# Who writes the high parts of the attention outputs: ScalarE in the place of VectorE

## The chip, the cores and the metric

One program on one core of a Trainium2 chip. The metric is the device time of one execution in microseconds; the number given is the median of several runs. All arrays are float32. One core has the engines TensorE (PE in the rows; PEld is its weight load), VectorE (DVE), ScalarE (ACT), GpSimd (POOL) and SyncE (SP, which here only issues DMAs). Each runs its own list of instructions in the order in which the program gives them, and waits for another engine only at a semaphore.

## The reference, cut to what matters

Two transformer blocks over 256 tokens of width 1024. There are five attentions; in the kernel they are called diff (8 heads of the differential attention), cross (4 heads of width 256 over a memory), mema (4 heads of width 64 over a second memory), swa (12 heads of width 64, sliding window of 128 with sinks) and memb (4 heads of width 64). Between cross and mema lies a layer that gathers experts, some 650 us long. What is touched here is the last step of four of the attentions and the product behind it:

```python
def cross_attention(h, m, w_cq, w_ckv, w_co):
    ...
    logits = jnp.einsum('bshd,bmhd->bhsm', q, k).astype(jnp.float32) * (CROSS_HEAD_DIM ** -0.5)
    p = jax.nn.softmax(logits, axis=-1).astype(v.dtype)
    o = jnp.einsum('bhsm,bmhd->bshd', p, v).reshape(b, s, CROSS_HEADS * CROSS_HEAD_DIM)
    return o @ w_co
...
        h = h + jnp.concatenate([main_out, mem_out], axis=-1) @ w_out[l]
```

## The kernel before

The large products run in a split form: an operand a is kept as a high part (its rounding to the fast matmul type) and a low part (a less its high part), and three products, high by high, low by high and high by low, are summed. The weights come in 154 halves of 1 MB; for each half ScalarE makes w_hi (L534) and VectorE w_lo (L1331). The operands' parts lie in op_hi and op_lo.

An attention is written as one loop in each of three engines, over items i (heads), two items ahead with the scores (lag 2; diff has lag 1). The lists of one turn i are, in this order:

- TensorE: scores S(i+2) (L1043), product with the values O(i-1) (L1056), transposed probabilities T(i) (L1079). O(i-1) needs the copy of T(i-1) in SBUF.
- VectorE: normalise(i) (in swa L1483, then L1484 and twice L1487), maxima(i+2) (L1439, or in swa twice L1436 and then L1447), in some turns a filler (a w_lo in cross; take_queries, L1859 and L1863, in turns 0 and 2 of swa), then take(i-1): a copy of O(i-1) to op_hi (L1506), a wait for that copy on VectorE's own semaphore, and the difference into op_lo (L1507), which also frees the bank.
- ScalarE: the exponentials exps(i+2) (in swa L604 first, then L609, two), which need maxima(i+2), then turned(i) (L622), the copy of T(i) out of its bank.

Behind the loop comes the last take on VectorE. O, S and T share four banks of PSUM in a rotation (misc_bank). The output product that follows (L961: co, outa, outb) starts when every O of the attentions in front of it has been taken. Its first two halves of w_hi and w_lo are made ahead; ScalarE makes the third w_hi after its last turned.

In cross an item is 128 partitions by 512 numbers, in the other three 64 partitions by 256. In mema, swa and memb two heads share a tile of op_hi, one in the lower 64 partitions and one in the upper. The diff attention goes to o_diff and is not split here.

Of the kernel before, what the change touches and what calls it, by code (L numbers as in the profile page):

```python
# [13 lines left out]
ACT = mybir.ActivationFunctionType  # L14
AX = mybir.AxisListType

P = 128
D = 1024
S = 256
# [3 lines left out]
HEADS = 8  # L23
HD = 64
# [7 lines left out]
SWA_HEADS = 12  # L32
SWA_TILES = SWA_HEADS * HD // P
MEM_HEADS = 4
# [145 lines left out]
def build(nc, x_in, mem_in, mem2_in, wstream, experts, vecs_in, bc_in, final_g, rel_in, keys_in, pool_in,  # L180
# [3 lines left out]
    with ctx:  # L184
# [5 lines left out]
        def sem(name):  # L190
            sems[name] = ctx.enter_context(nc.semaphore(name))
            return sems[name]
# [7 lines left out]
        op_hi = sb("op_hi", [P, 2, KC, S], F32R)  # L200
# [38 lines left out]
        o_diff = part(0, KC, S)  # L239
# [92 lines left out]
        gfin_in = sem("gfin_in")  # L332
        pool_in_s = sem("pool_in_s")
        alibi_in = sem("alibi_in")
        out_s = sem("out_s")
        dve_chain = sem("dve_chain")
        act_chain = sem("act_chain")
# [48 lines left out]
        def misc_bank(key):  # L386
            return banks[4 + MISC[key] % 4]
# [7 lines left out]
        def wait_misc(eng, key):  # L395
            eng.wait_ge(misc_full, MISC_ORDER[key] + 1)
# [4 lines left out]
        def empty_misc(ins, key):  # L401
            ins.then_inc(misc_free[MISC[key] % 4], 1)
# [27 lines left out]


        IN_PSUM = ("cross", "mema", "swa", "memb")

        def seen_keys(kind, qb):

# [2 lines left out]
        UNIT0, ITEM0 = {}, {}  # L438
# [79 lines left out]
        def _(act):  # L518
# [8 lines left out]
            def high_parts(upto):  # L527

                for n in range(halves[0], min(upto, NHALF)):
                    act.wait_ge(raw_in[n % RAW], 16 * (n // RAW + 1))  # L530

                    if n >= HI:
                        act.wait_ge(half_done, n - HI + 1)
                    act.activation(w_hi[:, n % HI, :, :], raw[:, n % RAW, :, :], ACT.Copy).then_inc(hi_ready, 1)  # L534
                halves[0] = max(halves[0], upto)
# [80 lines left out]
            def turned(kind, i):  # L616
                wait_misc(act, ("T", kind, i))

                if i >= 2:
                    wait_misc(act, ("O", kind, i - 2))  # L620
                n = S + seen_keys(kind, 0)
                e = act.activation(prob_t[:, (ITEM0[kind] + i) % 2, 0:n], misc_bank(("T", kind, i))[:, 0:n], ACT.Copy)  # L622
                empty_misc(e, ("T", kind, i))

            def free_prob(kind, i, group):

                j = i - 4 // group
                if j >= 0:
                    wait_misc(act, ("T", kind, j))

            def attention(kind, items, group, lag, fill=()):
                start = halves[0]
                for i in range(min(lag, items)):
                    for g in range(group):
                        exps(kind, i * group + g)
                for i in range(items):
                    if i + lag < items:
                        for g in range(group):
                            free_prob(kind, i + lag, group)
                            exps(kind, (i + lag) * group + g)  # L640
                    if i < len(fill):

                        high_parts(start + 2 * (i + 1))
                        if fill[i]:
                            fill[i]()
                    turned(kind, i)

            def copy_lin(key, dst, scale=None):
                product(key)
# [14 lines left out]
            for j in range(4):  # L664
                product(("q", j))
                src = lin_bank(("q", j)).rearrange("p (a b) -> p a b", a=2)
# [84 lines left out]
            for l in range(2):  # L751
                key = ("mkr", "ab"[l])
# [115 lines left out]
            for j in range(4):  # L868
                d = raw2[:, 2 * j:2 * j + 2, :]
# [439 lines left out]
        def _(dve):  # L1309
            def do(ins):  # L1310

                chain(dve, ins, dve_chain)
# [174 lines left out]
                    dve.tensor_scalar(prob[:, r, qb, 0:n], prob[:, r, qb, 0:n], rsum[:, r, qb:qb + 1], None,  # L1487
                                      ALU.mult).then_inc(p_ready, 1)

            def attention(kind, items, group, lag, extra, dst, fill=(), lows=()):  # L1490
                for i in range(min(lag, items)):
                    for g in range(group):
                        maxima(kind, i * group + g, **extra(i * group + g))
                def take(i):

                    key = ("O", kind, i)
                    wait_misc(dve, key)
                    lo, hi, buf, d, w = dst(i)
                    src = misc_bank(key)[lo:hi, 0:w]
                    if w == 2 * S:  # L1500
                        src = rows2(src)
                    if buf is None:
                        empty_misc(dve.tensor_copy(o_diff[:, d, :], src), key)
                        return

                    do(dve.tensor_copy(op_hi[lo:hi, buf, d, :], src))  # L1506
                    empty_misc(dve.tensor_tensor(op_lo[lo:hi, buf, d, :], src,  # L1507
                                                 op_hi[lo:hi, buf, d, :].bitcast(F32), ALU.subtract), key)

                for i in range(items):  # L1510
                    normalise(kind, i)
                    if i + lag < items:
                        for g in range(group):
                            u = (i + lag) * group + g
                            j = i + lag - 4 // group
                            if j >= 0:
                                wait_misc(dve, ("T", kind, j))
                            maxima(kind, u, **extra(u))
                    if i < len(lows):
                        low_parts(lows[i])  # L1520
                    if i < len(fill) and fill[i]:
                        fill[i]()
                    if i < len(lows) and kind == "diff":
                        low_parts(lows[i] + 1)
                    if i:
                        take(i - 1)
                take(items - 1)


# [47 lines left out]
            def take_cb(i):  # L1577
                def f():
                    for j in (2 * i, 2 * i + 1):
# [5 lines left out]
                return f  # L1585

            attention("diff", HEADS, 2, 1, lambda u: dict(bias_ap=bias[:, u // 2]),
                      lambda h: (0, P, None, h, S),
                      [take_cc(0), take_cc(1), take_cb(0), take_cb(1)],
                      [LAST[("cx", 3)] + 2 * i + 2 for i in range(HEADS)])  # L1590
            for j in range(4):
# [37 lines left out]
            for j in range(4):  # L1629
# [8 lines left out]
            add_and_take("mixo", "cross", "cross", 1)  # L1638
            low_parts(LAST[("cq", 3)])
            attention("cross", CROSS_HEADS, 1, 2, lambda u: {},  # L1640
                      lambda h: (0, P, 0, slice(2 * h, 2 * h + 2), 2 * S),
                      lows=[LAST[("cq", 3)] + 1, LAST[("cq", 3)] + 2])
            add_and_take("co", "ffn", "ffn", 1)

# [161 lines left out]
                                                        op_hi[:, 1, t, :].bitcast(F32), ALU.mult, ALU.subtract),  # L1806
                               key)

            def half_tile(t0):

                def f(h):
                    lo = HD * (h % 2)
                    return lo, lo + HD, 1, t0 + h // 2, S
                return f

            attention("mema", MEM_HEADS, 1, 2, lambda u: {}, half_tile(SWA_TILES))

            def slope_diagonals():
                for u, h in enumerate(SWA_ORDER):
# [50 lines left out]
            def swa_extra(u):  # L1870
                h = SWA_ORDER[u]
                return dict(sink=bc[:, 4 * HD + h:4 * HD + h + 1])

            low_parts(LAST[("inb", 3)] + 2)
            attention("swa", SWA_HEADS, 1, 2, swa_extra, half_tile(0),
                      [lambda: take_queries(2), None, lambda: take_queries(3)])
            attention("memb", MEM_HEADS, 1, 2, lambda u: {}, half_tile(SWA_TILES))
            mlp("b")


# [96 lines left out]
```

## Time and profile before

| | us |
|---|---|
| median of 3 runs | 1784.98 (1779.49 to 1786.22) |
| the profiled execution: its own time | 1784.74 |
| the profiled execution: span | 1782.9 |
| the stretch of cross, first scores to first output product | 412.5 to 435.15 |
| the stretch of mema | 1230.7 to 1247.4 |
| the stretch of swa and memb | 1504.7 to 1569.7 |

The profile is of one execution. A row of its timeline gives the start, the length, engine, line, operation, tile out and in, the shapes and the count; in square brackets stands how long the engine had been idle and what ended that. A row that says x2 or x4 covers several instructions that followed one another. The granted clock of TensorE is given as a part of 2.4 GHz; it has two levels, 1.2 and 2.4 GHz, and a mean between 0.5 and 1 is a mix of the two. The time that lies around the span is 1.84 us.

### The profile page before, as it was taken

The page shows a single profiled execution, that of the slowest core. Times are in us where ns is not written, and L with a number is a line of the kernel's source. Part 1 is how long each engine was busy: PE and PEld are TensorE (multiplying, and loading weights), DVE is VectorE, ACT ScalarE, POOL GpSimd, SP SyncE. Part 2 cuts the span into 40 slices and gives each one's busy share as a digit, 9 for nine tenths or more (in the row PEclk, how much of TensorE's full clock was granted, in tenths as well). Part 3 has the DMA queues.
Part 4 walks back from the last instruction along what each step waited for, and adds up shares of the span by engine and source line. Part 5 has one row for each costly group of instructions (what it writes and reads, how often), then busy time and mean ns, then how long its engine had stood idle before and what let it go on. Part 6 is the DMA issues. An engine that isn't in the chain of part 4 may idle for free.

```text
span 1782.9 us, 20788 instructions
## 1 busy us (share of the span) xinstructions
PE 1533.8 (86%) x7994; PEld 1149.3 (64%) x7994; DVE 1090.5 (61%) x1953; ACT 741.1 (42%) x1372; POOL 250.0 (14%) x271
## 2 busy tenths in 40 slices
PE   7999999998997877777777777776999998789998
PEld 7998989987872322223232222264899887679987
DVE  5468645854576666676766665457544558744454
ACT  5534555443443334333333333233454355445532
POOL 0000000000033333333333333200000000000000
PEclk9999999999999999999999999988999999899999
DMA  7743444452489999999999999921355644024563
GB/s 249 248 164 142 159 140 171 154 179 74 168 334 422 421 421 421 421 421 421 421 417 421 421 409 421 385 73 61 142 177 181 196 161 142 1 82 180 188 192 116
DMA packets 70738, 442.10 MB, mean 248 GB/s; under 512 B 6983, under 2 KB 9295, under 8 KB 25200
## 3 DMA queue, kind: packets, MB, share of 16 engines
q0 software_dynamic: 36864, 268.45, 36.3%
q1 hardware_dynamic: 29904, 163.59, 26.5%
q10 hardware_dynamic: 3872, 8.75, 1.4%
q8 instruction: 63, 1.03, 0.2%
q14 instruction: 35, 0.29, 0.0%
HBM read 439.70 MB, written 2.63 MB: 248 GB/s over the span
## 4 chain that ended last, share of the span: by engine, by line
PE 56%; DMA 24%; DVE 11%; ACT 5%; issue 3%; POOL 0%; ACTq 0%; SPq 0%; DVEq 0%; PEldq 0%; POOLq 0%
PE banks L932 27%; DMA arena<-experts,xn 24%; PE banks L961 16%; PE banks L1204 7%; DVE w_lo L1331 3%; DVE arena L1716 2%; PE banks L1056 1%; PE banks L998 1%; PE banks L1043 1%; ACT xn L804 1%; DVE arena L1859 1%; ACT xn L808 1%; ACT op_hi L559 1%; ACT xn L797 1%; ACT w_hi L534 1%
## 5 line engine op out<-in xcount | busy, mean ns | idle before, releaser
L1204 PE MATMUL banks<-arena,xn 128*128 128x512 f32 x1024 | 478.0, 611 | 159.2 <-ACT xn L808 159.2
L1331 DVE TENSOR_TENSOR w_lo<-raw,w_hi 128x2048 fp32r<-128x2048 f32 x154 | 352.2, 2289 | 262.0 <-PE banks L932 128.7
L1204 PEld LDWEIGHTS banks<-arena,xn 128*128 128x128 f32 x1024 | 187.1, 192 | 449.3 <-ACT xn L808 258.6
L1716 DVE CUSTOM_DVE_ANT_0 arena<-arena,banks 128x1024 f32<-128x1024 f32 x256 | 312.2, 1220 | 214.9 <-DMA arena<-experts,xn 214.7
L534 ACT ACTIVATE w_hi<-raw 128x2048 fp32r<-128x2048 f32 x154 | 293.3, 1911 | 160.9 <-PE banks L961 133.1
L509 POOL DMA_INDIRECT arena<-experts,xn x256 | 242.8, 948 | 437.6 <-PE banks L1204 385.5
L932 PE MATMUL banks<-op_hi,w_hi 128*128 128x256 f32 x1520 | 220.5, 287 | 2.5 <-ACT op_hi L559 2.5
L932 PE MATMUL banks<-op_hi,w_lo 128*128 128x256 f32 x1520 | 214.4, 284 | 8.6 <-DVE w_lo L1331 8.6
L932 PE MATMUL banks<-op_lo,w_hi 128*128 128x256 f32 x1520 | 214.1, 284 | 0.0
L797 ACT ACTIVATE xn<-xn,stat 128x2 f32<-128x2 f32 x128 | 37.8, 295 | 403.5 <-DVE xn L1716 400.3
L932 PEld LDWEIGHTS banks<-op_hi,w_hi 128*128 128x128 f32 x1520 | 197.8, 192 | 8.3 <-ACT op_hi L559 4.8
L932 PEld LDWEIGHTS banks<-op_hi,w_lo 128*128 128x128 f32 x1520 | 196.0, 192 | 10.2 <-DVE w_lo L1331 10.2
L932 PEld LDWEIGHTS banks<-op_lo,w_hi 128*128 128x128 f32 x1520 | 196.9, 193 | 0.0
L498 POOL TENSOR_TENSOR stat<-stat,small 128x2 f32<-128x2 f32 x10 | 6.9, 693 | 914.8 <-DVE stat L1349 914.8
L961 PE MATMUL banks<-w_hi,op_hi 128*128 128x512 f32 x448 | 122.1, 395 | 6.4 <-DVE op_lo L1507 4.3
L961 PE MATMUL banks<-w_lo,op_hi 128*128 128x512 f32 x448 | 121.9, 395 | 0.0
L961 PE MATMUL banks<-w_hi,op_lo 128*128 128x512 f32 x448 | 121.5, 393 | 0.0
L961 PEld LDWEIGHTS banks<-w_hi,op_hi 128*128 128x128 f32 x448 | 84.1, 190 | 25.0 <-issue 8.0
L961 PEld LDWEIGHTS banks<-w_hi,op_lo 128*128 128x128 f32 x448 | 85.4, 191 | 18.0
L961 PEld LDWEIGHTS banks<-w_lo,op_hi 128*128 128x128 f32 x448 | 85.3, 190 | 18.0
L808 ACT ACTIVATE xn<-consts,xn 128x128 f32<-128x128 f32 x256 | 88.7, 394 | 4.2
L654 ACT ACTIVATE arena<-banks 128x512 f32<-128x512 f32 x38 | 22.7, 597 | 101.7 <-PE banks L932 90.2
(210 smaller groups left out, 1198.8 us busy)
## 6 DMA issues: line engine op xcount, KB each, us to landing
raw<-wstream SPq DMA_DIRECT2D x154, 1024.0 KB, 5.1
arena<-experts,xn POOLq DMA_INDIRECT x256, 12.6
xn<-mem_in ACTq DMA_DIRECT2D x2, 1024.0 KB, 4.9
scratch<-scratch ACTq DMA_DIRECT2D x1, 1536.0 KB
x<-x_in SPq DMA_DIRECT2D x2, 512.0 KB, 4.4
arena<-scratch ACTq DMA_DIRECT2D x1, 1024.0 KB, 7.2
arena<-keys_in ACTq DMA_DIRECT2D x1, 1024.0 KB, 5.5
out_dram<-x SPq DMA_DIRECT2D x1, 1024.0 KB, 4.0
```

The source lines that it names most:

```text
L509: pool.indirect_dma_start(rows[:, k % GSLOTS, :], None, experts, bass.IndirectOffsetOnAxis(ap=expert[:, k // PAIRS, at:at + 1], axis=0))\
L534: act.activation(w_hi[:, n % HI, :, :], raw[:, n % RAW, :, :], ACT.Copy).then_inc(hi_ready, 1)
L559: e = act.activation(op_hi[:, buf, t, :], misc_bank(("xT", n, j))[:, f * S:(f + 1) * S], ACT.Copy, scale=gain(gain_)[:, t:t + 1])
L654: else act.activation(dst, src, ACT.Copy)
L797: act.activation(gact[:, s:s + 2], dots[:, s:s + 2], ACT.Gelu, scale=stats("ffn")[3][:, k // PAIRS:k // PAIRS + 1]).then_inc(gelu_ready, 1)
L804: act.activation(wact[:, s + e:s + e + 1], gact[:, s + e:s + e + 1], ACT.Copy, scale=weight[:, k // PAIRS, at:at + 1]).then_inc(wact_ready, 1)
L808: act.activation(diag[:, s + e, :], ident, ACT.Copy, scale=wact[:, s + e:s + e + 1])\
L932: mm = pe.matmul(lin_bank(key)[:, tokens_], l, m, start=start, stop=stop, skip_group_check=not (first and last))
L961: mm = pe.matmul(lin_bank(key), a[:, src, k0 + kc, tb * P:(tb + 1) * P], w[:, :, kc, :], start=start, stop=stop, skip_group_check=True)
L1204: mm = pe.matmul(sums[:, n, :], diag[:, s, :], rows[:, s, D + n * CW:D + (n + 1) * CW], start=False, stop=False, skip_group_check=True)
L1331: dve.tensor_tensor(w_lo[:, n % LO, :, :], raw[:, n % RAW, :, :], w_hi[:, n % HI, :, :].bitcast(F32), ALU.subtract).then_inc(lo_ready, 1)
L1716: dve.tensor_tensor_reduce(u, u, token_rows[k // PAIRS][:, :, :], 1.0, 0.0, ALU.mult, ALU.add, dots[:, s:s + 1]).then_inc(dot_ready, 1)
```

## The change

In cross, mema, swa and memb the copy of an O to op_hi is made by ScalarE (new function high_out), and VectorE makes only the difference. ScalarE issues high_out(i-1) behind turned(i), and the last one behind the loop. A new semaphore out_hi is raised by each; VectorE's take(i-1) waits for it in place of its own copy. The order of all other instructions is as it was. (The condition put before high_parts changes nothing: the four attentions have no fillers on ScalarE.)

```diff
@@ scalar
+            def high_out(kind, i):
+
+                key = ("O", kind, i)
+                wait_misc(act, key)
+                lo, hi, buf, d, w = out_place(kind, i)
+                src = misc_bank(key)[lo:hi, 0:w]
+                if w == 2 * S:
+                    src = src.rearrange("p (a b) -> p a b", a=2)
+                act.activation(op_hi[lo:hi, buf, d, :], src, ACT.Copy).then_inc(out_hi, 1)
+
...
                     turned(kind, i)
+                    if i and kind != "diff":
+                        high_out(kind, i - 1)
+                if kind != "diff":
+                    high_out(kind, items - 1)
@@ vector
                     key = ("O", kind, i)
                     wait_misc(dve, key)
...
-                    do(dve.tensor_copy(op_hi[lo:hi, buf, d, :], src))
+                    dve.wait_ge(out_hi, outs_made(kind, i))
...
                     empty_misc(dve.tensor_tensor(op_lo[lo:hi, buf, d, :], src,
                                                  op_hi[lo:hi, buf, d, :].bitcast(F32), ALU.subtract), key)
@@ shared
+        def out_place(kind, i):
+
+            if kind == "cross":
+                return 0, P, 0, slice(2 * i, 2 * i + 2), 2 * S
+            lo = HD * (i % 2)
+            return lo, lo + HD, 1, (0 if kind == "swa" else SWA_TILES) + i // 2, S
+
+        def outs_made(kind, i):
+
+            return ITEM0[kind] - HEADS + i + 1
```

## Rows read from the trace of the kernel before

**Rows 1.** The page's first part, the engines' busy time over the whole span.

```profile
PE 1533.8 (86%) x7994; PEld 1149.3 (64%) x7994; DVE 1090.5 (61%) x1953; ACT 741.1 (42%) x1372; POOL 250.0 (14%) x271
```

**Rows 2.** The timeline of swa's turns, from turn 3 to turn 10 (start, length, instruction).

```profile
1526.66 0.16 DVE L1483 TENSOR_TENSOR ssum<-ssum,esink 128x2 f32<-128x2 f32 x1
...
1540.96 0.14 DVE L1483 TENSOR_TENSOR ssum<-ssum,esink 128x2 f32<-128x2 f32 x1
1542.46 0.23 DVE L1447 TENSOR_SCALAR nmax<-nmax,bc 128x2 f32<-128x2 f32 x1
1543.00 0.43 DVE L1506 CAST op_hi<-banks 64x256 fp32r<-64x256 f32 x1 [0.32 <-PE banks L1056]
1543.46 0.43 DVE L1507 TENSOR_TENSOR op_lo<-banks,op_hi 64x256 fp32r<-64x256 f32 x1
1543.92 0.16 DVE L1483 TENSOR_TENSOR ssum<-ssum,esink 128x2 f32<-128x2 f32 x1
1545.56 0.23 DVE L1447 TENSOR_SCALAR nmax<-nmax,bc 128x2 f32<-128x2 f32 x1
1545.88 0.29 ACT L604 ACTIVATE esink<-nmax,bc 128x2 f32<-128x2 f32 x1 [1.48 <-DVE nmax L1447]
1546.47 0.14 DVE L1483 TENSOR_TENSOR ssum<-ssum,esink 128x2 f32<-128x2 f32 x1
1547.01 0.49 ACT L622 ACTIVATE arena<-banks 128x384 f32<-128x384 f32 x1
```

**Rows 3.** ScalarE's copies of T out of the banks (L622), all of them.

```profile
L622 ACT ACTIVATE arena<-banks x32: 486/490/597, 128.6 to 1566.6; 128x384 f32<-128x384 f32 x20, 128x512 f32<-128x512 f32 x12
```

**Rows 4.** The timeline of swa's second and third turns.

```profile
1518.34 0.49 ACT L622 ACTIVATE arena<-banks 128x384 f32<-128x384 f32 x1
...
1520.66 0.23 DVE L1447 TENSOR_SCALAR nmax<-nmax,bc 128x2 f32<-128x2 f32 x1
```

**Rows 5.** The timeline of swa's last turns.

```profile
1546.85 0.55 DVE L1487 TENSOR_SCALAR arena<-arena,rsum 128x128 f32<-128x128 f32 x2
...
1547.55 0.92 PE L1056 MATMUL banks<-arena 128*128 128x256 f32 x4 [1.85 <-ACT arena L622]
...
1552.25 1.65 PE L1056 MATMUL banks<-arena 128*128 128x256 f32 x4 [0.58 <-ACT arena L622]
```

**Rows 6.** The timeline of mema.

```profile
1236.10 0.66 PE L1079 MATMUL banks<-consts,arena 128*128 128x128 f32 x4 [0.39 <-DVE arena L1487]
...
1239.84 0.60 ACT L622 ACTIVATE arena<-banks 128x512 f32<-128x512 f32 x1 [0.44 <-PE banks L1079]
...
1242.10 0.60 ACT L622 ACTIVATE arena<-banks 128x512 f32<-128x512 f32 x1 [1.66 <-PE banks L1079]
...
1242.58 0.17 DVE L1484 RECIPROCAL rsum<-ssum 128x2 f32<-128x2 f32 x1
...
1242.78 0.62 DVE L1487 TENSOR_SCALAR arena<-arena,rsum 128x256 f32<-128x256 f32 x2
```

**Rows 7.** The timeline of cross.

```profile
422.48 2.29 DVE L1331 TENSOR_TENSOR w_lo<-raw,w_hi 128x2048 fp32r<-128x2048 f32 x1
...
423.69 0.59 ACT L622 ACTIVATE arena<-banks 128x512 f32<-128x512 f32 x1
...
427.57 0.60 ACT L622 ACTIVATE arena<-banks 128x512 f32<-128x512 f32 x1 [3.29 <-PE banks L1079]
...
430.69 0.60 ACT L622 ACTIVATE arena<-banks 128x512 f32<-128x512 f32 x1 [2.52 <-PE banks L1079]
```

**Rows 8.** Stretches: length, busy PE, PEld, DVE, ACT, POOL (counts), granted clock, DMA.

```profile
1238.00:1247.30 9.30, 5.83 (x28) 4.21 (x28) 5.19 (x15) 4.79 (x9) 0.00 (x0) 1.00 0.01 2
...
1560.00:1569.60 9.60, 5.83 (x28) 4.21 (x28) 5.45 (x15) 5.05 (x9) 0.00 (x0) 1.00 0.00 1
1569.60:1574.00 4.40, 4.32 (x12) 3.50 (x13) 0.00 (x0) 0.00 (x0) 0.00 (x0) 0.61 0.00 0
```

**Rows 9.** The timeline of TensorE, the first output matmuls behind memb.

```profile
1569.68 2.04 PE L961 MATMUL banks<-w_hi,op_hi 128*128 128x512 f32 x4 [1.29 <-DVE op_lo L1507]
```

More of the change, by code:

```diff
@@ L334, in build @@
         alibi_in = sem("alibi_in")
+        out_hi = sem("out_hi")
         out_s = sem("out_s")
@@ L641, in attention @@
                     if i < len(fill):
-                        high_parts(start + 2 * (i + 1))
+                        if kind == "diff":
+                            high_parts(start + 2 * (i + 1))
                         if fill[i]:
@@ L1488, in normalise, with attention @@
                                       ALU.mult).then_inc(p_ready, 1)
-            def attention(kind, items, group, lag, extra, dst, fill=(), lows=()):
+            def attention(kind, items, group, lag, extra, fill=(), lows=()):
                 for i in range(min(lag, items)):
@@ L1497, in take @@
                     wait_misc(dve, key)
-                    lo, hi, buf, d, w = dst(i)
+                    if kind == "diff":
+                        empty_misc(dve.tensor_copy(o_diff[:, i, :], misc_bank(key)[:, 0:S]), key)
+                        return
+                    dve.wait_ge(out_hi, outs_made(kind, i))
+                    lo, hi, buf, d, w = out_place(kind, i)
                     src = misc_bank(key)[lo:hi, 0:w]
@@ L1501, in take @@
                         src = rows2(src)
-                    if buf is None:
-                        empty_misc(dve.tensor_copy(o_diff[:, d, :], src), key)
-                        return
-                    do(dve.tensor_copy(op_hi[lo:hi, buf, d, :], src))
                     empty_misc(dve.tensor_tensor(op_lo[lo:hi, buf, d, :], src,
@@ L1587, in _ @@
             attention("diff", HEADS, 2, 1, lambda u: dict(bias_ap=bias[:, u // 2]),
-                      lambda h: (0, P, None, h, S),
                       [take_cc(0), take_cc(1), take_cb(0), take_cb(1)],
@@ L1640, in _ @@
             attention("cross", CROSS_HEADS, 1, 2, lambda u: {},
-                      lambda h: (0, P, 0, slice(2 * h, 2 * h + 2), 2 * S),
                       lows=[LAST[("cq", 3)] + 1, LAST[("cq", 3)] + 2])
@@ L1807, in _ @@
                                key)
[L1809 to L1816, printed above, removed]
+            attention("mema", MEM_HEADS, 1, 2, lambda u: {})
             def slope_diagonals():
@@ L1874, in _ @@
             low_parts(LAST[("inb", 3)] + 2)
-            attention("swa", SWA_HEADS, 1, 2, swa_extra, half_tile(0),
+            attention("swa", SWA_HEADS, 1, 2, swa_extra,
                       [lambda: take_queries(2), None, lambda: take_queries(3)])
-            attention("memb", MEM_HEADS, 1, 2, lambda u: {}, half_tile(SWA_TILES))
+            attention("memb", MEM_HEADS, 1, 2, lambda u: {})
             mlp("b")
```

## Prediction, made before the changed kernel was run

> **What bounds the kernel now.** I read the page first. TensorE is busy 86% of the span, VectorE 61%, ScalarE 42% [rows 1], but these are means over stages, and the change touches three short ones: cross, mema, and swa with memb. So I went on with the timeline of each, and read it for one thing: in which order the three engines hand an item to one another. In swa VectorE sets the pace. Its list for one turn begins with L1483 at 1540.96, at 1543.92 and at 1546.47, so two turns took 5.51 us, and between the turn that begins at 1526.66 (turn 3) and the one at 1546.47 (turn 10) lie 19.81 us, 2.83 for each of the 7 [rows 2]. ScalarE meanwhile stood idle for 1.48 us before it got the maxima it needed [rows 2], so it has room for more work. That is the case for the change. What it says nothing about is the order of the hand-overs. In mema from turn 1 on, and in cross, the pace is set by a ring of TensorE and ScalarE: turned (L622), O (L1056), T (L1079), turned; in mema it takes 2.26 us, from 1239.84 to 1242.10 [rows 6], in cross 3.88 and 3.12 [rows 7]. VectorE's takes lie beside that ring.
>
> **What the change removes.** 24 copies on VectorE, 20 of 0.43 us and 4 wider ones. In swa a copy and the start of the difference behind it are 0.46 us apart (1543.00 and 1543.46) [rows 2].
>
> **What it adds: the copy on ScalarE.** No such copy of 64x256 is in the trace. The nearest row is ScalarE's copy out of the banks (L622): 0.49 us for 384 numbers a partition and 0.60 for 512 [rows 3], so 0.11 for 128 numbers and 0.38 for 256. I take 0.38, since the operation is the same and only the width differs; above I bound it by the 0.49 of the wider copy. It follows turned directly. Consecutive ScalarE instructions overlap by about 0.1 us in the timeline, so it begins 0.39 + 0.02 after turned does, and ends 0.79 us after turned began (in mema and memb, where turned takes 0.60, 0.90 us; in cross, with 0.60 for the copy too, 1.10).
>
> **What it adds: a wait that closes a ring.** take(i-1) on VectorE now waits for high_out(i-1). ScalarE issues that behind turned(i), turned(i) behind exps(i+2), and exps(i+2) waits for maxima(i+2), which VectorE has only just made. Behind the waiting instruction on VectorE is queued normalise(i+1), for which T(i+1) on TensorE waits, and maxima(i+3). So one turn of swa becomes a ring with no overlap:
> - from L1483 to the end of L1447 on VectorE: 1.87 us when the turn followed a wait of VectorE (1543.92 to 1545.79), 1.73 when it did not (1540.96 to 1542.69) [rows 2]; the new turns all follow a wait, so 1.87;
> - hand-over to ScalarE: 1545.79 to 1545.88, 0.09 [rows 2];
> - exps up to the start of turned: 1545.88 to 1547.01, 1.13 [rows 2];
> - turned and high_out: 0.79, as above;
> - hand-over to VectorE: 0.04, an estimate from the 0.09 just read and the 0.02 to 0.04 of the shorter ones in the timelines;
> - the difference, up to the next L1483: 1543.46 to 1543.92, 0.46 [rows 2].
>
> The sum is 4.38 us (4.24 with 1.73; 4.49 with a copy of 0.49), against 2.83. TensorE is not late in it: T(i) is made some 1.5 us after the turn began, turned asks for it at 3.1.
>
> **swa, summed.** Turns 3 to 9: 7 x 4.38 = 30.7 against 19.8, +10.8 us (+9.9 with the low bound, +11.6 with the high). Turns 0 and 2 carry take_queries behind their maxima, some 5 us of VectorE work, and that hides the wait. Turn 1 doesn't: turned began at 1518.34, so low(0) starts at 1519.17, the next turn at 1519.63, and its maxima end at 1521.50 where they ended at 1520.89 [rows 4], +0.6; turn 2 then saves its copy, 0.46. Together +0.1. The tail, from turn 10's L1483 to the end of the last O, took 7.43 us (1546.47 to 1553.90) [rows 2, 5]. There are no exps in it. New: normalise 0.93 (1546.47 to 1547.40) [rows 2, 5], 0.06 to TensorE, T 0.50 (three of the matmuls of which four take 0.66 [rows 6]), 0.04, then 0.79 + 0.04 + 0.46 to the next turn, once more 0.93 + 0.06 + 0.50 + 0.04, turned 0.49, 0.05, and O 0.92: 5.8 us, a gain of 1.6. But O, which took 0.92 us at 1547.55, took 1.65 at 1552.25 [rows 5], as TensorE had half its clock there; with that O, and two T longer by the same ratio (0.40 each, an estimate), it is 7.3, a gain of 0.1. TensorE will have paused more, not less, so I take the second. swa: +0.1 + 10.8 - 0.1 = +10.8.
>
> **mema and memb.** Turns 0 and 1 are as before, since take(0) comes after normalise(1). From turned(1) to turned(2) the new ring is 0.90 + 0.04 + 0.46, then normalise 0.82 (1242.58 to 1243.40), 0.06, T after a pause 0.66, 0.04: 2.98 us, against 2.26 [rows 6]. This ring is run twice, to turned(3), so +1.4 us. At the end ScalarE's copy and VectorE's copy are the same step by either engine. memb has the same instructions: +1.4.
>
> **cross.** turned(1) began at 423.69, so low(0) could start at 424.83; VectorE is with a w_lo until 424.77 [rows 7], so here the wait is covered, and the copy saved. normalise(2) is ready 0.5 us sooner, and turned(2) comes at about 427.05 where it came at 427.57 [rows 7]. To turned(3) it is then 1.10 + 0.04 + 0.69 + 0.82 + 0.06 + 0.6 + 0.04 = 3.35 in place of 3.12 [rows 7]. cross: -0.3.
>
> **What follows each stage.** ScalarE now makes the third w_hi after the last high_out, 2 us later; the first two halves of the output product are ready and keep TensorE busy for some 10 us, which covers it. The weight DMAs wait for VectorE's w_lo alone, which keeps its place. So a delay of the attention is passed on whole, as the product waits for the last take. The banks' rotation gives nothing: the bank of O(i-1) is next wanted by T(i+1), which comes after it anyway.
>
> **TensorE's clock.** In mema TensorE was busy 5.83 of 9.30 us, 63%, and kept the full clock behind it too. In memb it was busy 5.83 of 9.60, 61%, at the full clock, and the stretch behind it had a mean clock of 0.61 [rows 8]. With 1.4 us more mema is at 54%, below what was followed by the fall. I therefore add one restart at half clock behind mema. Its price: at a mean of 0.61, 0.78 of the 4.40 us ran at half [rows 8], 3.4 us for 1.7 us of full-clock work; so 1.7 us at most, nothing at least. I take 1.6. (Behind memb, and by the timeline behind cross, it is there already.) The Trainium skill, "TensorE: Matmul & The Clock Gate", section "HAM oscillation — how this bites in real kernels", puts such falls down to long pauses of the engine in which it waits for data. The trace speaks against that as the only cause: the pause in front of the fall behind memb was 1.29 us [rows 9]. By the page's rule nothing would be added, and the sum would be 1.6 less.
>
> **The sum.** -0.3 + 1.4 + 10.8 + 1.4 + 1.6 = +14.9 us. The profiled execution took 1784.74, 0.2 less than the median, so both give 1799.6. With every low bound (9.9 and the full tail gain, no clock) it is 1784.7 - 0.3 + 1.4 + 8.4 + 1.4 = 1795.6; with the copy at 0.49 it is 1800.4.
>
> **The rivals.**
> - Faster: the copy is gone and the wait costs nothing. This is the change as its words have it. It decides where high_out(i-1) ends before VectorE has made maxima(i+2) and its fillers. Then 8 copies of 0.46 us leave VectorE's path in swa, and little elsewhere: 1784.7 - 3.7 = 1781. For it: ScalarE's idle time [rows 2], and turns 0 and 2 of swa and turn 1 of cross, where a filler covers the wait. Against it: in all other turns ScalarE can't even begin the exps in front of high_out before the maxima are done, so VectorE waits at least 0.09 + 1.13 + 0.79 + 0.04 = 2.05 us. Chance 0.05.
> - No change that can be told: the wait bites only in every second turn, as the copy's wait for O does now (turns of 2.96 and 2.55 us [rows 2]), since VectorE's queue runs on meanwhile. Then a pair of turns takes 4.38 + 2.55, swa grows by 4.4 us, and the whole by 6.9 with nothing for the clock: 1791.6. Against it: the count that take waits for is that of its own item, so no turn escapes. Chance 0.09.
> - Slower still: TensorE falls to half its clock within swa's turns and in mema and memb. Its busy time in a turn of swa would be some 2.5 us of 4.4. Then each T and O on the path costs 0.40 and 0.73 more [rows 5]; two T and one O in mema and again in memb, 3.1 together, and, as an estimate, 2 us for scores that come late: 1804.7. Chance 0.12.
>
> **How the numbers follow.** Forecast 1799.6 with chance 0.74. 0.5%, about what a measurement of this kernel can tell from no change, is 8.9 us, so slower means above 1793.9. The forecast and the slow rival lie there: 0.86; same 0.09; faster 0.05. The range is 1793 to 1805: the low end is the bound 1795.6 less 2.6 us for the spread of the runs, the high end takes in most of the slow rival.
>
> **What would show it.** In swa after: a turn of 4.4 us, VectorE idle some 2 us before each L1507 and released there by ScalarE's new copy, and that copy 0.38 us long. In mema: L622 to L622 of 3.0 us. In cross: the output product at 434.9 in place of 435.15. If VectorE's idle time before L1507 is short, or ScalarE's copy stands before the exps, I am wrong. If the spacing is right and the total is not, look at the granted clock behind mema and in swa.

## The result, and the profile after

The changed kernel took 1792.53 us (median; 1791.95 to 1792.68) where the kernel before took 1784.69: a ratio of 1.0051, 95% interval [1.0037, 1.0065]. In a second comparison it took 1792.59 us against 1783.52, ratio 1.0056 [1.0041, 1.0071]. It is slower, by 8 to 10 us; I had forecast 14.9. As a time it lies 0.5 us below my range (1793.0 to 1805.0); as a ratio to the median I started from it would be 1794.

VectorE did lose work, 1090.5 us [rows 1] to 1079.5, and ScalarE gained 8.4:

```profile
PE 1530.5 (85%) x7994; PEld 1143.9 (64%) x7994; DVE 1079.5 (60%) x1929; ACT 749.5 (42%) x1396; POOL 249.7 (14%) x271
```

What came in its place is in the view of VectorE's difference (L1507 before, L1533 after; ScalarE's new copy is L645, its exponentials are L616 and L621, turned is L634): its 24 instructions, and how long VectorE had stood idle before them.

```profile
L1533 DVE TENSOR_TENSOR op_lo<-banks,op_hi x24: 416/428/693, 424.9 to 1577.7; 64x256 fp32r<-64x256 f32 x20, 128x512 fp32r<-128x512 f32 x4
...
  ACT op_hi L645: 41.5, 22
```

22 of the 24 waited for ScalarE's copy, 41.5 us in all, which is not all loss, since part of it was idle time before as well. The timeline of one turn of swa shows the ring (start, length, instruction; the first and the last row are the starts of turns 6 and 7):

```profile
1536.36 0.14 DVE L1509 TENSOR_TENSOR ssum<-ssum,esink 128x2 f32<-128x2 f32 x1
...
1537.85 0.23 DVE L1473 TENSOR_SCALAR nmax<-nmax,bc 128x2 f32<-128x2 f32 x1
...
1538.17 0.29 ACT L616 ACTIVATE esink<-nmax,bc 128x2 f32<-128x2 f32 x1 [2.26 <-DVE nmax L1473]
...
1539.31 0.49 ACT L634 ACTIVATE arena<-banks 128x384 f32<-128x384 f32 x1
1539.82 0.38 ACT L645 ACTIVATE op_hi<-banks 64x256 fp32r<-64x256 f32 x1
...
1540.30 0.43 DVE L1533 TENSOR_TENSOR op_lo<-banks,op_hi 64x256 fp32r<-64x256 f32 x1 [2.22 <-ACT op_hi L645]
1540.76 0.16 DVE L1509 TENSOR_TENSOR ssum<-ssum,esink 128x2 f32<-128x2 f32 x1
```

VectorE makes the maxima, then stands idle for 2.22 us while ScalarE does the exponentials, turned and the copy, and only then goes on. ScalarE in its turn stood idle for 2.26 us before the exponentials. Each waits for the other once a turn, and a turn takes 4.40 us; the one before it took 4.27. From turn 3 to turn 10 it is 30.30 us, against 19.81 [rows 2]:

```profile
1523.41 0.16 DVE L1509 TENSOR_TENSOR ssum<-ssum,esink 128x2 f32<-128x2 f32 x1
...
1553.71 0.14 DVE L1509 TENSOR_TENSOR ssum<-ssum,esink 128x2 f32<-128x2 f32 x1
```

In mema, turned to turned was 2.26 us [rows 6]; after it is 2.84 and 3.13:

```profile
1236.81 0.60 ACT L634 ACTIVATE arena<-banks 128x512 f32<-128x512 f32 x1 [0.44 <-PE banks L1105]
...
1239.65 0.60 ACT L634 ACTIVATE arena<-banks 128x512 f32<-128x512 f32 x1 [1.99 <-PE banks L1105]
...
1242.78 0.60 ACT L634 ACTIVATE arena<-banks 128x512 f32<-128x512 f32 x1 [2.13 <-PE banks L1105]
```

To see the whole, I cut the timelines of TensorE at the first scores and the first output matmul of each stage. The table has all executions that were profiled (us; the run names are those of the experiments below). "Behind cross" is the first 100 us behind it, up to a matmul of the layer that gathers experts (L1204 before, L1230 after); "behind mema" goes up to swa, and "behind memb" up to the last matmul:

| run | cross | mema | swa | memb | behind cross | behind mema | behind memb | span |
|---|---|---|---|---|---|---|---|---|
| before | 22.66 | 16.70 | 48.96 | 15.99 | 100.44 | 257.35 | 207.58 | 1782.9 |
| before (c_before2) | 22.66 | 16.70 | 48.92 | 16.02 | 99.34 | 257.20 | 206.02 | 1778.3 |
| before (c_before3) | 22.66 | 16.70 | 48.93 | 15.99 | 100.88 | 257.35 | 207.52 | 1784.5 |
| after | 22.34 | 18.18 | 59.43 | 17.46 | 98.97 | 255.76 | 206.00 | 1790.1 |
| after (c_after2) | 22.33 | 18.19 | 59.45 | 17.97 | 99.01 | 257.42 | 205.99 | 1793.9 |
| after (c_after3) | 22.33 | 18.18 | 59.44 | 17.45 | 98.68 | 255.76 | 205.99 | 1790.4 |
| e1_copy_first | 22.51 | 17.45 | 49.04 | 16.94 | 98.66 | 258.99 | 206.01 | 1784.0 |
| e2_no_copy | 21.21 | 16.40 | 45.47 | 14.64 | 98.75 | 257.43 | 205.99 | 1773.2 |
| e3_double | 23.51 | 18.99 | 61.86 | 18.87 | 98.95 | 257.37 | 205.98 | 1797.6 |
| e4_swa_old | 22.34 | 18.18 | 48.91 | 17.47 | 98.78 | 255.78 | 206.00 | 1779.3 |
| e5_late_take | 21.87 | 16.72 | 52.76 | 15.23 | 98.98 | 257.27 | 207.60 | 1782.7 |
| e6_shift | 22.66 | 16.70 | 48.94 | 15.98 | 100.72 | 257.18 | 206.00 | 1783.0 |
| e7_shift_twice | 22.66 | 16.69 | 48.90 | 15.99 | 98.95 | 257.09 | 206.01 | 1781.4 |
| e8_cross_late | 21.90 | 16.85 | 48.89 | 16.02 | 98.74 | 257.12 | 206.01 | 1777.3 |

The four stages grew from 104.3 to 117.4 us, +13.1, and the same again in every execution to within 0.6 us. The span of the two first traces grew by 7.2 only. The other 5.9 came back outside the stages, where the instructions are the same ones: 1.5 behind cross, 1.6 behind mema, 1.6 behind memb, and 1.3 in the rest of the expert layer, which the table doesn't hold (695.1 us before, 693.8 after).

### The profile page after: what moved, and what is told of

It is laid out like the page before. It is cut to its first block, busy times and chain, and to the rows that moved or that the text cites. A ratio compares the mean times of both kernels' runs of the same rounds, so it can differ in the third digit from the quotient of the medians.

```text
span 1790.1 us, 20812 instructions
## 1 busy us (share of the span) xinstructions
PE 1530.5 (85%) x7994; PEld 1143.9 (64%) x7994; DVE 1079.5 (60%) x1929; ACT 749.5 (42%) x1396; POOL 249.7 (14%) x271
## 4 chain that ended last, share of the span: by engine, by line
PE 55%; DMA 24%; DVE 11%; ACT 6%; issue 3%; POOL 0%; ACTq 0%; DVEq 0%; SPq 0%; PEldq 0%; POOLq 0%
PE banks L958 27%; DMA arena<-experts,xn 23%; PE banks L987 16%; PE banks L1230 7%; DVE w_lo L1357 2%; DVE arena L1740 2%; PE banks L1024 1%; PE banks L1082 1%; ACT xn L830 1%; PE banks L1069 1%; DVE arena L1876 1%; ACT op_hi L571 1%; ACT xn L834 1%; ACT arena L621 1%; ACT xn L823 1%
## 5 line engine op out<-in xcount | busy, mean ns | idle before, releaser
L1230 PE MATMUL banks<-arena,xn 128*128 128x512 f32 x1024 | 475.0, 608 | 161.9 <-ACT xn L834 161.9
L1230 PEld LDWEIGHTS banks<-arena,xn 128*128 128x128 f32 x1024 | 185.8, 191 | 450.2 <-ACT xn L834 262.1
## 6 DMA issues: line engine op xcount, KB each, us to landing
arena<-experts,xn POOLq DMA_INDIRECT x256, 13.3
```

The lines of the kernel that those rows point to most:

```text
L1230: mm = pe.matmul(sums[:, n, :], diag[:, s, :], rows[:, s, D + n * CW:D + (n + 1) * CW], start=False, stop=False, skip_group_check=True)
```

## The experiments

**The two kernels again.** How much of that 5.9 us belongs to the change?

> The kernel before, once more, for a second trace of it. If the stretches at half clock behind cross and behind memb are tied to the kernel, both are there again, the first output matmul rows are long (2.0 us for four behind memb), and the time is 1784 to 1786. If they are chance, they lie elsewhere or are missing, and the time moves by some 1.5 us for each. The time from the end of cross to the start of mema was 795.5 us in the first trace; if that is stable, it is within 0.5 us of it.

> The kernel before, a third trace. The stretch from the first output matmul behind mema to swa's first scores took 255.8 us in three executions (of different kernels) in which it began 1236.3 to 1237.0 us behind the first matmul, and 257.2 to 259.0 us in six in which it began earlier or later. Theory place in time: it is long again if it begins near 1235.4 or 1238.4, as in the first two traces. Theory tied to the change: long in any case.

> The changed kernel once more. Tied to the kernel: no half clock behind cross, mema and memb again, 792.8 us from the end of cross to mema, 1792 to 1793 in all. Chance: some of them return, and the time moves by about 1.5 us for each. The stages themselves are expected to repeat within 0.3 us (cross 22.3, mema 18.2, swa 59.4, memb 17.5).

> The changed kernel in five rounds, for the size of the loss. The four stages grew by 13.1 us together in the two traces of it (swa 10.5, mema 1.5, memb 1.5 to 2.0, cross -0.3), and all else differed between executions of one and the same kernel by up to 4.7 us with the stretches at half clock. Theory chance (those stretches have nothing to do with the change): over many runs the difference nears 13 us less what the clock gives by luck, a ratio of 1.006 to 1.0075. Theory tied (the longer stages really cost fewer restarts elsewhere): it stays at 8 to 9 us, a ratio of 1.0045 to 1.005.

Measured: 1780.14 and 1786.35 us for the kernel before, 1795.76 and 1792.59 (median of 5) for the changed one. The stages repeat to 0.05 us, but for memb in c_after2 (17.97 for 17.46). The stretch from the end of cross to mema, which I had expected to repeat, doesn't: it took 795.5, 792.3 and 795.9 us in the three traces before, and 792.8, 792.2 and 792.6 in the three after. Much of what moves is where TensorE has half its clock. Of the three traces of the kernel before, before and c_before3 show it behind cross, and c_before2 doesn't. First the windows view (stretch, length, busy times, then the granted clock) and the timeline of the first trace:

```profile
435.10:440.00 4.90, 4.85 (x14) 3.87 (x15) 0.00 (x0) 0.00 (x0) 0.00 (x0) 0.65 0.00 0
```

```profile
435.15 1.17 PE L961 MATMUL banks<-w_hi,op_hi 128*128 128x512 f32 x4 [1.82 <-DVE op_lo L1507]
```

Then the same two views of c_before2:

```profile
435.20:440.00 4.80, 4.47 (x20) 3.71 (x21) 0.00 (x0) 0.00 (x0) 0.00 (x0) 1.00 0.00 0
```

```profile
435.53 1.17 PE L961 MATMUL banks<-w_hi,op_hi 128*128 128x512 f32 x4 [1.82 <-DVE op_lo L1507]
```

One kernel, one stage of 22.66 us, one pause of 1.82 us, and once 0.65, once 1.00. So a restart at half clock there is no property of the kernel alone.

Behind mema the half clock that separates 257.3 from 255.8 us doesn't lie at the stage. It lies over 200 us later, in 32 small matmuls (L998 before, L1024 after) in front of which TensorE paused for 3.17 us. The windows and the timeline of the kernel before:

```profile
1455.00:1462.00 7.00, 5.10 (x31) 5.13 (x32) 4.42 (x9) 4.26 (x9) 0.69 (x1) 0.76 0.24 76
```

```profile
1456.90 5.44 PE L998 MATMUL banks<-arena,x 128*128 128x128 f32 x32 [3.17 <-DVE arena L1370]
```

And of the changed kernel:

```profile
1453.00:1460.00 7.00, 4.51 (x38) 4.34 (x38) 5.37 (x12) 5.79 (x12) 0.69 (x1) 1.00 0.20 67
```

```profile
1455.39 3.81 PE L1024 MATMUL banks<-arena,x 128*128 128x128 f32 x32 [3.17 <-DVE arena L1396]
```

The same pause, and 5.44 us or 3.81 for the same matmuls. All eleven executions with 257 us or more have half clock at this place, and the three with 255.8 don't. Right behind mema the clock fell in one of the fourteen, e1_copy_first, which has it at both places and takes 259.0.

But the table is lopsided: behind cross the five executions with the old cross took 99.0 to 100.9 us, mean 100.1, and the nine in which cross differs 98.7 to 99.0. Behind memb two of the three traces of the kernel before show 207.5, and none of the changed one. The three "behind" columns sum to 564.6 on average over the three traces before and 561.2 over the three after, so 3.4 us were given back in these stretches. The larger comparison fits that: 13.1 less 3.4 is 9.7, and the medians differ by 9.1. In c_after3's expectation I named two theories, 1.006 to 1.0075 for chance and 1.0045 to 1.005 for a real saving elsewhere; 1.0056 lies between them, and its interval reaches into both.

The times of all executions say more than the single traces. The 55 executions of the kernel before that were timed beside the experiments fall into two groups: 24 from 1779.5 to 1782.3 us, with a mean granted clock of 0.982, and 31 from 1783.4 to 1787.0 us, with 0.978. Of the 11 of the changed kernel nine took 1791.9 to 1792.7 us (granted clock 0.979 to 0.982) and two 1795.8 and 1796.0 us (0.978 and 0.977). Group against group the change costs some 11 us (11.5 and 11.0 by the means). The medians differ by only 7.8 and 9.1, as the median of the kernel before lies in its upper group and that of the changed kernel in its lower one.

c_before3 was to tell two theories of the stretch behind mema apart, one that it depends on when the stretch begins, one that it is tied to the change. It began 1240.1 us behind the first matmul and took 257.35, which fits both.

**The copy at the head of ScalarE's turn.** Same copies, another place.

```diff
                 for i in range(items):
+                    if i and kind != "diff":
+                        high_out(kind, i - 1)
                     if i + lag < items:
...
                     turned(kind, i)
-                    if i and kind != "diff":
-                        high_out(kind, i - 1)
```

> ScalarE's copy of O(i-1) stands at the head of ScalarE's turn i, ahead of exps(i+2) and turned(i), in place of behind turned(i). Theory ring (the loss comes from where the copy stands: behind the exps, which wait for the maxima that VectorE has just made): the ring is then turned 0.49 + 0.05 + O 0.92 + 0.04 + copy 0.38 + exps 1.13 = 3.0 us in swa against 4.3 in the changed kernel and 2.83 before, mema and memb are as before, cross is 0.3 shorter; the whole is 1785 to 1787, ratio to before 1.000 to 1.002. Theory load (each ScalarE copy and its two hand-overs cost the same wherever they stand): no better than the changed kernel, 1792, ratio 1.004 to 1.005.

Measured: 1785.09 us, ratio 1.0012 [1.0001, 1.0023]; swa 49.04 us, 10.4 less than in the changed kernel, with every copy still on ScalarE. The timeline of swa (copy, turned, O, copy of the next turn, and one turn further):

```profile
1532.40 0.38 ACT L645 ACTIVATE op_hi<-banks 64x256 fp32r<-64x256 f32 x1 [1.01 <-PE banks L1082]
...
1533.94 0.49 ACT L634 ACTIVATE arena<-banks 128x384 f32<-128x384 f32 x1
...
1534.48 0.92 PE L1082 MATMUL banks<-arena 128*128 128x256 f32 x4 [0.48 <-ACT arena L634]
...
1535.43 0.38 ACT L645 ACTIVATE op_hi<-banks 64x256 fp32r<-64x256 f32 x1 [1.01 <-PE banks L1082]
...
1538.34 0.38 ACT L645 ACTIVATE op_hi<-banks 64x256 fp32r<-64x256 f32 x1 [1.01 <-PE banks L1082]
```

The ring is now the one expected, over O and the exponentials, 3.03 and 2.91 us a turn for the expected 3.0. The load theory is out: it is the place of the copy, not the copy. A miss: I expected mema and memb as before, and they took 0.75 and 0.95 us more. In mema's timeline the copy of O(0) (1238.64) now stands ahead of the last exponentials, which wait with it for O(0): from turned(0) at 1236.82 to turned(1) at 1239.82 it takes 3.00 us, where the kernel before took 2.25. The next two turns take 2.24 and 2.25 as before. In all, the four stages are 1.6 us longer than before.

**No copy at all** (from the kernel before; the line of VectorE's copy is taken out).

```diff
-                    do(dve.tensor_copy(op_hi[lo:hi, buf, d, :], src))
```

> The kernel before with VectorE's copy to op_hi left out in the four attentions; the high parts are then what stood there earlier, so the output projections behind the attentions are computed from wrong high parts. It prices what the change takes off VectorE if nothing came in its place. Theory ring: two turns of swa are one ring (nmax, exps, turned, O, copy, difference, normalise, maxima) of 5.51 us with one copy of 0.46 in it, so 5.05 for two, 1.6 us less over seven turns, and 0.46 to 0.7 less at the end of each attention: 3 to 4 us in all, ratio 0.998. If VectorE's load alone set the pace, each turn would lose 0.46: 5.5 us less, ratio 0.997.

Measured: 1775.74 us, ratio 0.9959 [0.9945, 0.9972]. Seven turns of swa took 18.07 us in its timeline (1522.91 to 1540.98) for 19.81, so 1.7 less as the ring of two turns has it. But swa as a whole lost 3.5 us, cross 1.45 and memb 1.35, 6.6 in all: nearly double what I had expected. Much of the rest is TensorE's clock, and not the copies. In the kernel before swa's last two O took 1.65 us each at half clock [rows 5], and memb's first twelve score matmuls 3.88; here they took 0.92 and 2.75:

```profile
1544.34 0.92 PE L1056 MATMUL banks<-arena 128*128 128x256 f32 x4 [0.58 <-ACT arena L622]
...
1546.17 0.92 PE L1056 MATMUL banks<-arena 128*128 128x256 f32 x4 [0.58 <-ACT arena L622]
1546.92 2.75 PE L1043 MATMUL banks<-memk,arena 128*128 128x256 f32 x12
```

That is up to 2 x 0.73 + 1.13 = 2.6 us, and leaves some 4, the upper end of the expected 3 to 4. The copies of cross (0.69 us each, queued ahead of normalise), of which I had counted only the last, are among these 4; no run took them apart. So 6.6 us is more than VectorE's copies cost by themselves, and an upper bound of what the change could gain in the stages.

**Every ScalarE copy twice.**

```diff
+        spare = part(9472, 2, 384)
...
+                n = min(w, 384)
+                act.activation(spare[lo:hi, (ITEM0[kind] + i) % 2, 0:n], misc_bank(key)[lo:hi, 0:n],
+                               ACT.Copy).then_inc(out_hi, 1)
                 act.activation(op_hi[lo:hi, buf, d, :], src, ACT.Copy).then_inc(out_hi, 1)
...
-            return ITEM0[kind] - HEADS + i + 1
+            return 2 * (ITEM0[kind] - HEADS + i + 1)
```

> Each ScalarE copy is done twice, first to an unused place, then to op_hi (in cross the first is 384 numbers wide). Theory ring: each turn that waits grows by one start-to-start of such a copy, 0.28 us: swa by 3.1 us (11 of them), mema and memb by 0.85 each, cross by up to 0.9; 5 to 6 us over the changed kernel, a ratio to before of 1.009 to 1.0105. If the copies lay in ScalarE's idle time and only the hand-overs cost, the ratio stays that of the changed kernel.

Measured: 1801.23 us, ratio 1.0105 [1.0089, 1.0122]. Stages: cross +1.2, mema +0.8, swa +2.4, memb +1.4 over the changed kernel, 5.8 in all for the expected 5 to 6. The parts are off in both directions: cross and memb grew by more than the 0.9 and 0.85 I gave them, swa by less than 3.1. In memb part of it is again the clock, since its first twelve score matmuls took 4.78 us, where the changed kernel's took 3.67. Turns 3 to 10 of swa took 32.19 us (1527.35 to 1559.54) for 30.30, 0.27 a turn for the expected 0.28. In the timeline the two copies start 0.26 us apart, and VectorE waits for the second:

```profile
1530.45 0.49 ACT L635 ACTIVATE arena<-banks 128x384 f32<-128x384 f32 x1
1530.82 0.37 ACT L647 ACTIVATE arena<-banks 64x256 f32<-64x256 f32 x1
1531.08 0.37 ACT L649 ACTIVATE op_hi<-banks 64x256 fp32r<-64x256 f32 x1
1531.55 0.42 DVE L1537 TENSOR_TENSOR op_lo<-banks,op_hi 64x256 fp32r<-64x256 f32 x1 [2.34 <-ACT op_hi L649]
```

So the second copy adds to each turn what lies between the starts of the two, on an engine that is busy 42% of the time: the copy is on the path.

**swa as before, the rest changed.** In swa high_out is left out, and VectorE copies.

```diff
-            return ITEM0[kind] - HEADS + i + 1
+            return ITEM0[kind] - HEADS + i + 1 - (SWA_HEADS if kind == "memb" else 0)
...
-                    if i and kind != "diff":
+                    if i and kind not in ("diff", "swa"):
                         high_out(kind, i - 1)
-                if kind != "diff":
+                if kind not in ("diff", "swa"):
                     high_out(kind, items - 1)
...
-                    dve.wait_ge(out_hi, outs_made(kind, i))
+                    if kind != "swa":
+                        dve.wait_ge(out_hi, outs_made(kind, i))
...
+                    if kind == "swa":
+                        do(dve.tensor_copy(op_hi[lo:hi, buf, d, :], src))
```

> The change in cross, mema and memb only; swa as before. Theory ring: swa is back at 49.0 us while cross stays at 22.3, mema at 18.2 and memb at 17.5; the whole is 2.6 us over before, ratio 1.0015 (1.0005 to 1.0025). If the loss were spread over all copies alike (20 small ones, 13 us), half the small copies are still moved and 5 to 6 us would stay, ratio 1.003.

Measured: 1782.52 us, ratio 0.9999 [0.9989, 1.0009]. The stages are as expected to 0.1 us, swa 48.91; the loss of the change sits in swa, 10.5 of 13.1 us. A miss is the total, which is below my expected interval: the stages are 2.6 us longer than before, and the stretches behind them 4.0 us shorter (560.6 to the mean of 564.6).

**The difference one turn later.** The copies stay on ScalarE where the change has them.

```diff
-                    if i:
-                        take(i - 1)
+                    late = 1 if kind == "diff" else 2
+                    if i >= late:
+                        take(i - late)
+                if kind != "diff":
+                    take(items - 2)
                 take(items - 1)
```

> The changed kernel with VectorE's difference put off by one turn: take(i-2) in place of take(i-1) behind maxima(i+2), so the copy it waits for was issued a whole turn earlier. Theory ring: VectorE no longer waits in the turn in which it made the maxima. What is left in swa is a ring over TensorE, since T(i) needs the bank of O(i-2): difference 0.43, 0.06, T 0.39, S(i+3) 1.48, maxima 0.89, together 3.25 us a turn; swa 51 to 52 us, mema 16.7, memb 16.0, cross 22.3; 2 to 3 us over before in all, ratio 1.001 to 1.002. Theory load: as the changed kernel, ratio 1.005 to 1.007.

Measured: 1785.76 us, ratio 1.0013 [1.0004, 1.0022]. The timeline of a turn and a half of swa (difference, T, scores, maxima, difference):

```profile
1531.19 0.41 DVE L1533 TENSOR_TENSOR op_lo<-banks,op_hi 64x256 fp32r<-64x256 f32 x1
...
1531.75 0.52 PE L1105 MATMUL banks<-consts,arena 128*128 128x128 f32 x3 [0.80 <-DVE op_lo L1533]
...
1532.11 1.48 PE L1069 MATMUL banks<-arena 128*128 128x128 f32 x8
...
1533.69 0.62 DVE L1462 TENSOR_REDUCE nmax<-banks 128x1 f32<-128x128 f32 x2 [1.23 <-PE banks L1069]
...
1534.61 0.43 DVE L1533 TENSOR_TENSOR op_lo<-banks,op_hi 64x256 fp32r<-64x256 f32 x1
```

In this stretch VectorE no longer waits for ScalarE. T waits for the bank that the difference frees, and the maxima for the scores: 3.42 us a turn for the expected 3.25, swa 52.76 for 51 to 52, mema 16.72 as expected, cross 21.87 for 22.3, memb 15.23 for 16.0 (its first twelve score matmuls took 2.76 us, at full clock). The four stages are 2.3 us longer than before. With e1 this is the second way to break the ring, by moving the waiter and not the copy.

**A pure delay** (from the kernel before; e7_shift_twice has range(2) and so does the reciprocal twice). It asks whether the time given back depends on when the stages come.

```diff
             dve.wait_ge(gfin_in, 16)
+            idle = win[:, 1, 0, 0:192]
+            do(dve.memset(idle, 1.0))
+            for _ in range(1):
+                do(dve.reciprocal(idle, idle))
```

> The kernel before, with a pure delay of some 1.5 us on VectorE ahead of the last scaling of the first block (one memset and one reciprocal of a part of the arena that is overwritten later), long before mema. Theory place in time: the stages keep their lengths of before, and where the stretch behind mema now begins between 1236.3 and 1237.0 it takes 255.8 us, so that the delay is given back. Theory tied to the change: 257.3 us and a time 1.5 us longer.

> As e6_shift, with two reciprocals, a delay of some 2.8 us. Theory place in time: the start of the stretch behind mema moves on by another 1.3 us, and it takes 255.8 or 257.3 us by whether it begins in the short or in the long places; the two shifted kernels differ in more or less than the 1.3 us they were given. Theory tied: 257.3 us in both.

Measured: 1784.84 and 1783.22 us. The delay was really there (0.22 and 1.35 us in the first, 0.22 and 2.74 in the second, on VectorE with TensorE idle). The stretch behind mema began 1240.3 and 1238.8 us behind the first matmul and took 257.2 and 257.1 us. Neither fell into the 1236.3 to 1237.0 where the three short ones began, so these two runs don't decide; c_after2 began at 1238.6 and took 257.4 although it is the changed kernel, which speaks against "tied to the change". It fits the place in time, but doesn't show it. That a delay of 1.6 us gives a time in the middle of the kernel before's spread shows how little a single execution says here.

**Only cross, and there the later difference.** The parts that paid, put together: high_out and its wait in cross alone, with take(i-2); the other three as before.

```diff
-                    if i and kind != "diff":
+                    if i and kind == "cross":
                         high_out(kind, i - 1)
-                if kind != "diff":
+                if kind == "cross":
                     high_out(kind, items - 1)
...
-                    dve.wait_ge(out_hi, outs_made(kind, i))
+                    if kind == "cross":
+                        dve.wait_ge(out_hi, outs_made(kind, i))
...
+                    if kind != "cross":
+                        do(dve.tensor_copy(op_hi[lo:hi, buf, d, :], src))
...
-                    if i:
-                        take(i - 1)
+                    late = 2 if kind == "cross" else 1
+                    if i >= late:
+                        take(i - late)
+                if kind == "cross":
+                    take(items - 2)
                 take(items - 1)
```

> The best parts only: in cross ScalarE's copies and the difference put off by one turn, in mema, swa and memb the kernel before. Theory ring: cross 21.9 us as in e5_late_take (22.7 before), the others 16.7, 49.0 and 16.0; 0.8 us less in all, a ratio of 0.9995, which the measurement can't tell from 1.

Measured: 1779.78 us against 1783.77, ratio 0.9982 [0.9972, 0.9993]: faster than both kernels. Cross is 21.90 us, 0.76 less, as expected. The first output matmul starts at 434.39 for 435.15:

```profile
434.39 1.16 PE L987 MATMUL banks<-w_hi,op_hi 128*128 128x512 f32 x4 [1.82 <-DVE op_lo L1536]
```

The ratio stands for 3.2 us, where I had expected 0.8, too little to tell: the stage gives 0.76, and the stretch behind cross takes 98.74 us for a mean of 100.1. So once more a part of it lies outside the stage, in the clock as far as the traces behind cross show it.

## Why the prediction was right, and where it was not

- **The ring of swa**, the step on which all rested: 4.38 us a turn forecast, 4.33 measured, alternating between 4.27 and 4.40. 30.7 us for seven turns forecast, 30.30 measured. e1, e3 and e5 show that it is the ring: break it at the copy and it is gone, break it at the waiter and it is gone, lengthen the copy and each turn grows by it.
- **The copy on ScalarE**: 0.38 us from the line through two wider copies, 0.38 in the row. It started 0.51 us behind turned in every second turn (1539.31 to 1539.82), 0.1 later than I had put it, and 0.37 behind it in the others.
- **Turns 0 to 2**: +0.1 forecast. From swa's first scores to turn 3 it was 21.94 us and is 21.83, -0.1. **The tail**: 7.3 us forecast, 7.5 measured (turn 10 to the end of the last O), with O at 1.65 us as I had chosen. That clock belongs to an execution too: with no copy at all these O took 0.92.
- **mema and memb**: +1.4 each forecast, +1.5 each measured; the two rings of mema 2.84 and 3.13 us for 2.98.
- **cross**: -0.3 forecast and measured. The output product starts at 434.88 for the forecast 434.9.
- **The stages' sum**: -0.3 + 1.4 + 10.8 + 1.4 = +13.3 forecast, +13.1 measured.
- **TensorE's clock** is the step that failed, and with it the size. I added 1.6 us for a restart at half clock behind mema, since TensorE's busy share there would fall below that of memb. The changed kernel has the full clock behind mema, as the kernel before had, and the full clock behind memb too, where the kernel before had 0.61 [rows 8]:

```profile
1245.80:1250.20 4.40, 4.38 (x19) 3.65 (x20) 0.00 (x0) 1.11 (x1) 0.00 (x0) 1.00 0.00 0
...
1578.50:1582.90 4.40, 4.40 (x20) 3.62 (x20) 0.00 (x0) 1.02 (x1) 0.00 (x0) 1.00 0.01 4
```

  In place of +1.6 the three stretches behind the stages gave -3.4 on average over three traces each, and the difference of the two is 5.0 us, nearly all of what I was off by (14.9 for 9 to 10). My reason, the lower busy share in mema, was answered by those rows: mema did get longer by 1.5 us, and no fall followed it in any of the three traces. The stretch behind mema gained or lost its 1.6 us elsewhere, at the pause of 3.17 us over 200 us later, a place that I had not looked at. The page's rule that I weighed (the Trainium skill, "TensorE: Matmul & The Clock Gate", section "HAM oscillation — how this bites in real kernels": long pauses make the clock fall) would have put 0 behind mema and the whole at 1798, closer. By itself it doesn't give the traces either: behind cross the same pause of 1.82 us went with 0.65 and with 1.00, and the same pause of 3.17 us with 0.76 and with 1.00. What I should have done is to put the clock into the range on both sides, since one trace can't tell a fall that belongs to the kernel from one that happened in that execution.
- **The rivals.** Faster is out: VectorE waited in 22 of 24 takes, and even with no copy at all the stages were only 6.6 us shorter. "Every second turn" is out: the turns of 4.27 and 4.40 both hold a wait of 2.1 to 2.2 us. Its total, 1791.6, came near the measured one by accident. Slower still is out for swa's steady turns, though TensorE did run at half clock in some of them (0.84 on average from 1526 to 1556): they keep their 4.27 and 4.40 us.
- **Still open**: what decides in which executions TensorE restarts at half clock, and so whether the 3.4 us belong to the change. Shown is that the restarts differ between executions of one kernel, that in the three stretches of the table they are fewer in the kernels whose cross differs from the kernel before, and that nine of 11 executions of the changed kernel lie in its lower group of times against 24 of 55 of the kernel before. That speaks for a real saving, but names no cause. The two delays that were to settle it missed the place.

## What to carry to other kernels

Work moved to an idle engine can cost, besides its own length, the wait for what stands in front of it in that engine's list: here 0.38 us of work, put behind exponentials that wait for the very engine that then waits for it, closed a ring of two engines and cost 1.5 us a turn. Before moving an instruction, follow the list of the new engine back from it until a wait, and ask whether what that wait needs is made just before the point where the result is wanted. If so, move the instruction ahead of that wait, or move the waiter back by a turn: here that left 1.6 and 2.3 us of the 13.1 that the stages had lost.

## What was not expected of the hardware

Executions of one kernel spread by 7 us (1779.5 to 1787.0 in all its runs), with the stages repeating to 0.05 us but for memb in one trace. A restart at half clock is worth some 1.6 us: the stretch behind memb takes 206.0 or 207.5 us and that behind mema 255.8 or 257.3 (once 259.0), with nothing between the two values in fourteen executions. That such steps make up much of the spread of a kernel was new to me. They aren't all of it: from the first matmul to the first scores of cross the same instructions took 403.6 to 405.9 us in the six traces of the two kernels, and the traces weren't asked why. Nor does a step have to lie at the instructions that were changed, as the one behind mema shows.
